# Latent attentions: value products in two parts over neighbouring tiles, values in three equal pieces, a key projection moved by one tile

## The chip, the cores and the metric

The kernel runs on one NeuronCore of a Trainium2 chip. What is compared is the time of one execution on the device, in microseconds (us). The figure for the kernel before is the median of three runs; the rows below come from one further execution, taken with the hardware profiler.

## The reference

A sequence of 1,024 tokens, with 16 meta tokens ahead of it (1,040 positions, padded here to 1,044), passes two layers of a first block and then one layer of a second block. Only the latent attention of the first block is touched by the change. Cut to what matters:

```python
def mla_mix(c_q, c_kv, k_r, ...):                 # 4 heads
    q = (rms_norm(c_q, q_norm_w) @ w_uq)          # per head 128 plain + 64 rotated columns
    kv = (rms_norm(c_kv, kv_norm_w) @ w_ukv)      # per head 128 key + 128 value columns
    k_nope, v = kv[..., :128], kv[..., 128:]
    k = concatenate([k_nope, broadcast(k_rope)])
    s = einsum('bqhd,bkhd->bhqk', q, k) * scale
    p = softmax(s)
    o = einsum('bhqk,bkhd->bqhd', p, v)           # the value product
for l in range(2):
    ...
    y_a = mla_mix(...)
    mix = concatenate([y_f * silu(f_gate), y_p * silu(p_gate), y_a * silu(a_gate)])
    h = h + mix @ w_out[l]
```

Everything is float32 in accuracy. A product of two float32 operands is made of three products of rounded parts, high by high, high by low and low by high; hence the names that end in `_hi` and `_lo`.

## The kernel before, in words

The function `latent_heads` (L1414) computes the attention of a layer. It is called once for each of the two layers and fills about a sixth of the program. The work is cut into tiles of 116 query rows (`HT`), 9 tiles to a head (`NH`), 4 heads, so 36 tiles to a layer. A chunk is 3 tiles, 348 positions (`CH1`); projections and value products are made chunk by chunk.

What each engine does for a tile `s` is written out by hand, in one loop over `s` on each engine. Each engine works off its own list strictly in the order written; semaphores tie the lists together.

- **TensorE** (`PE`): `score(s)` (L1468) makes 15 products for the scores of tile `s` over all keys, into three PSUM banks that exist once. Its first product waits until the exponential of the tile before has read them (`exp_done`). Then come the jobs of the tile (below), then `transposes(s - 1)` (L1515), 9 transposes of the probabilities of the tile before, again into three banks that exist once: they wait for `turned_saved`, which says that the last transposed tile has been copied out.
- **ScalarE** (`ACT`): the exponential of tile `s` (L1543), the high parts of the jobs' results (L1553 to L1559), then the high part of the transposed probabilities of tile `s - 1` (`pT_hi`, L1576).
- **VectorE** (`DVE`): the maximum of the scores of tile `s` and its negative (L1586, L1588), the rotation of query parts (L1594 to L1597), the reciprocal and the scaling of the probabilities (L1600, L1602), the low parts of the jobs' results (L1620) or, for a value product, its multiplication by the gate (L1608, tile `mix`, for the last head `last`), then the low part of the transposed probabilities (`pT_lo`, L1631).

A layer has 60 jobs beside the tiles: `kn` (a key projection of one chunk, 2 float32 products), `qn` and `qr` (plain and rotated query projection, 3 products each), `v` (values, several tiles of keys at a time), and `pv` (the value product of a chunk: 9 tiles of keys, 3 products each, 27 in all). `head_jobs` (L1386) is the table that gives the jobs of the tile with index `i` in head `n`. All jobs share two PSUM banks, 6 and 7, in turn; job `j` may start only when job `j - 2` has been saved (L1489, L1490):

```python
if j >= 2:
    pe.wait_ge(job_saved, j - 1)
```

The transposed probabilities of a chunk stand in one buffer, which exists once. ScalarE may write the first tile of the next chunk into it only when the value product of the last chunk has been made (L1574, L1575), where `x` is the tile whose transposes are copied out:

```python
if x % 3 == 0 and x:
    act.wait_ge(job_done, number["pv", (x - 1) // NH, (x - 1) % NH // 3] + 1)
```

`x` is 3 and 6 (index in the head) in the loop passes of tiles 4 and 7, where the table also has the value products of chunks 0 and 1. Chunk 2's stands in tile 1 of the next head.

Of the kernel before, what the change touches and what calls it, by code (L numbers as in the profile page):

```python
# [29 lines left out]
P = 128  # L30
# [16 lines left out]
MLA_HEADS = 4  # L47
MLA_SCALE = (128 + 64) ** -0.5
HALF = L1 // 2 + 1
HT = 116  # L50
NH = TP // HT
# [1334 lines left out]
def head_jobs(s):  # L1386


    n, i = divmod(s, NH)
    jobs = {0: [("kn", n + 1, 0), ("kn", n + 1, 1)], 1: [("pv", n - 1, 2)], 2: [("v", n, 0), ("v", n, 1)],  # L1390
            3: [("v", n, 2), ("qr", n, 2)], 4: [("qn", n, 2), ("pv", n, 0)], 5: [("qr", n + 1, 0)],
            6: [("qn", n + 1, 0)], 7: [("kn", n + 1, 2), ("pv", n, 1)], 8: [("qr", n + 1, 1), ("qn", n + 1, 1)]}
    return [job for job in jobs[i] if 0 <= job[1] < MLA_HEADS]


# [18 lines left out]
def latent_heads(core, io, layer, slots, mix, rope, wqk, ident, tensors, first_tile):  # L1414
# [4 lines left out]
    nc = core.nc  # L1419
    tiles = MLA_HEADS * NH  # L1420
    steps = range(-NH, tiles + 2)
    order = [job for s in steps for job in head_jobs(s)]
    number = {job: j for j, job in enumerate(order)}
    with_hi = [sum(job[0] != "pv" for job in order[:j]) for j in range(len(order) + 1)]
    ropes = [sum(job[0] == "qr" for job in order[:j]) for j in range(len(order) + 1)]

    t = tensors
# [13 lines left out]
        return (3 * n + c) % 2  # L1441

    def v_tiles(c):
        return slice(4 * c, min(4 * c + 4, NH))

    def v_bank(j, c):
        n = min(4, NH - 4 * c)
        return core.psum[0:HT, 6 + j % 2, 0:n * P].rearrange("p (t n) -> p t n", t=n)
    with core.phase("pads_set", "wqk_in2", "wqk_in3", "job_done", "job_hi", "job_saved", "qr_step",
                    "qr_ready", "scores_done", "max_ready", "bias_ready", "exp_done", "inv_done", "prob_ready",  # L1450
                    "turned_done", "turned_hi", "turned_saved") as \
# [11 lines left out]
        @block.tensor  # L1463
        def _(pe):
            def score(s):
                n, i = divmod(s, NH)
                if s == 0:
                    pe.wait_ge(pads_set, 1)  # L1468
                if i == 0:
                    pe.wait_ge(job_saved, number["kn", n, 2] + 1)  # L1470
                if i % 3 == 0:
                    pe.wait_ge(job_saved, max(number["qn", n, i // 3], number["qr", n, i // 3]) + 1)
                if s >= 1:
                    pe.wait_ge(exp_done, s)
                b = slot_of(n, i // 3)
                q = slice(i % 3 * HT, (i % 3 + 1) * HT)
                for part, (one, other) in enumerate((
                        (qn_hi[:, b, q], kn_hi[n % 2]), (qn_hi[:, b, q], kn_lo[n % 2]),
                        (qn_lo[:, b, q], kn_hi[n % 2]), (qr_both[:, b, q], kr_hi),
                        (qr_both[:, b, q], kr_lo))):  # L1480
                    for c in range(3):
                        w = min(CH1, L1 - c * CH1)
                        last = nc.tensor.matmul(scores[:, c, 0:w], one, other[:, c * CH1:c * CH1 + w],
                                                start=(part == 0), stop=(part == 4))
                last.then_inc(scores_done, 1)

            def work(job):
                kind, n, c = job
                j = number[job]  # L1489
                if j >= 2:  # L1490
                    pe.wait_ge(job_saved, j - 1)
                if kind == "kn" and c == 0 and n >= 2:
                    pe.wait_ge(wqk_in[n], 16)
                if kind == "pv":
                    pe.wait_ge(turned_saved, NH * n + 3 * c + 3)
                    pe.wait_ge(job_saved, number["v", n, 2] + 1)
                    for t in range(NH):
                        for part, (one, other) in enumerate(((v_hi, pT_hi), (v_hi, pT_lo), (v_lo, pT_hi))):
                            last = nc.tensor.matmul(bank(j), one[:, t, :], other[:, t, :],
                                                    start=(t == 0 and part == 0), stop=(t == NH - 1 and part == 2))  # L1500
                elif kind == "v":
                    for t in range(4 * c, min(4 * c + 4, NH)):
                        for k in range(2):
                            last = nc.tensor.matmul(core.psum[0:HT, 6 + j % 2, t % 4 * P:(t % 4 + 1) * P],
                                                    slots[:, CKV + k, t * HT:(t + 1) * HT],
                                                    wqk[n % 2][:, 3 + k, 128:256], start=(k == 0), stop=(k == 1))
                else:
                    k0, src, kt = (3, CKV, 2) if kind == "kn" else (0, CQ, 3)
                    cols = slice(128, 256) if kind == "qr" else slice(0, 128)
                    for k in range(kt):  # L1510
                        last = nc.tensor.matmul(bank(j), wqk[n % 2][:, k0 + k, cols], slots[:, src + k, chunk(c)],  # L1511
                                                start=(k == 0), stop=(k == kt - 1))
                last.then_inc(job_done, 1)

            def transposes(s):  # L1515
                pe.wait_ge(prob_ready, s + 1)
                if s >= 1:
                    pe.wait_ge(turned_saved, s)
                for t in range(NH):
                    last = nc.tensor.transpose(core.psum[0:HT, 3 + t // 3, t % 3 * HT:(t % 3 + 1) * HT],  # L1520
                                               prob[s % 2][:, t * HT:(t + 1) * HT], ident[0:HT, 0:HT])
                last.then_inc(turned_done, 1)
            for s in steps:
                if 0 <= s < tiles:
                    score(s)
                if s == tiles:
                    pe.wait_ge(exp_done, tiles)
                    first_tile.tensor(pe, range(0, 2))
                if s == tiles + 1:
                    first_tile.tensor(pe, range(2, 4))  # L1530
                for job in head_jobs(s):
                    work(job)
                if 1 <= s <= tiles:
                    transposes(s - 1)

        @block.scalar
        def _(act):
            for s in steps:
# [7 lines left out]
                for job in head_jobs(s):  # L1546
                    kind, n, c = job
                    j = number[job]
                    if kind != "pv":
                        act.wait_ge(job_done, j + 1)  # L1550
                    if kind == "qr":
                        act.wait_ge(qr_ready, ropes[j] + 1)
                        nc.scalar.activation(qr_both[0:64, slot_of(n, c), :], qa[:], ACT.Copy).then_inc(job_hi, 1)  # L1553
                    if kind == "qn":
                        nc.scalar.activation(qn_hi[:, slot_of(n, c), :], bank(j), ACT.Copy).then_inc(job_hi, 1)
                    if kind == "kn":
                        nc.scalar.activation(kn_hi[n % 2][:, chunk(c)], bank(j), ACT.Copy).then_inc(job_hi, 1)
                    if kind == "v":
                        nc.scalar.activation(v_hi[:, v_tiles(c), :], v_bank(j, c), ACT.Copy).then_inc(job_hi, 1)  # L1559
# [20 lines left out]
        def _(dve):  # L1580
            nc.vector.memset(core.psum[:, 2, L1 - 2 * CH1:CH1], MASKED).then_inc(pads_set, 1)
            for s in steps:
# [6 lines left out]
                for job in head_jobs(s):  # L1589
                    kind, n, c = job  # L1590
                    j = number[job]
# [11 lines left out]
                for job in head_jobs(s):  # L1603
                    kind, n, c = job
                    j = number[job]
                    if kind == "pv":
                        dve.wait_ge(job_done, j + 1)
                        nc.vector.tensor_tensor(mix[:, 4 + n, chunk(c)], bank(j), slots[:, A_GATE + n, chunk(c)],  # L1608
                                                ALU.mult).then_inc(job_saved, 1)
                        continue  # L1610
                    dve.wait_ge(job_hi, with_hi[j] + 1)
                    if kind == "qr":
                        lo, x, hi = (qr_both[64:P, slot_of(n, c), :], qa[:], qr_both[0:64, slot_of(n, c), :])
                    if kind == "qn":
                        lo, x, hi = qn_lo[:, slot_of(n, c), :], bank(j), qn_hi[:, slot_of(n, c), :]
                    if kind == "kn":
                        lo, x, hi = kn_lo[n % 2][:, chunk(c)], bank(j), kn_hi[n % 2][:, chunk(c)]
                    if kind == "v":
                        lo, x, hi = v_lo[:, v_tiles(c), :], v_bank(j, c), v_hi[:, v_tiles(c), :]
                    nc.vector.tensor_tensor(lo, x, hi.bitcast(F32), ALU.subtract).then_inc(job_saved, 1)  # L1620
# [3027 lines left out]
```

## Time and profile before

| what | value |
|---|---|
| median of 3 runs | 3171.22 us (3167.86 to 3183.21) |
| the profiled execution, its own time | 3170.96 us |
| its span in the profile | 3169.2 us |
| granted TensorE clock over the span | 0.984 of 2.4 GHz |
| the four heads of layer 1 in the trace | 281.5 to about 537 us |
| the four heads of layer 2 in the trace | about 888 to 1146 us |

Times in the rows are microseconds from the start of the span. TensorE's pass over an operand has two records, the load of the weights (PEld) and the product (PE); products are pipelined, so that one of 0.32 us follows the one before it by about half of that, and the beginnings, not the durations, are to be subtracted. What stands in brackets at a row's end is the idle time of the engine before it, and what ended it. PEclk is the share of full clock that was granted.

### The profile page before, as it was taken

The numbers are of one execution on the slowest core, as the hardware profiler recorded it, in microseconds if no ns is written. First come the engines' busy times: TensorE is split into PE (matmuls) and PEld (weight loads), VectorE is DVE, ScalarE is ACT, GpSimd is POOL, SyncE is SP. The second block draws the span as 40 slices with busy tenths as digits, with TensorE's granted clock in tenths as the row PEclk, the third lists the DMA queues.
The fourth block names the chain that finished last, engine by engine and source line by source line (L and its number), as shares of the span: only waits on it lengthen the run. The fifth ranks groups of instructions, "written<-read, shape, count | busy, mean of one in ns | idle before, by whom it ended". The sixth has DMA issues, their size and how long they took to land. (4 is left out here: it accounts for less than half of the span.)

```text
span 3169.2 us, 44449 instructions
## 1 busy us (share of the span) xinstructions
PE 2997.3 (95%) x18182; PEld 2558.4 (81%) x18182; DVE 2117.7 (67%) x2634; ACT 1067.5 (34%) x1555; POOL 961.7 (30%) x656
## 2 busy tenths in 40 slices
PE   7999998999999989998999898898999999999997
PEld 7997888999878888887876776666777886888875
DVE  5535765444366645998927756777957767877798
ACT  2012333201133423322012322666315453344534
POOL 2320000333100012553322532111333443454575
PEclk9999999999999999999999999999999999999998
DMA  4111000111100002433333004222533543555543
GB/s 143 45 36 43 23 1 7 62 61 47 55 9 23 1 21 67 149 117 114 103 129 125 8 35 117 75 67 71 208 131 97 189 158 119 163 166 173 163 149 120
DMA packets 114818, 284.38 MB, mean 90 GB/s; under 512 B 15238, under 2 KB 20998, under 8 KB 114600
## 3 DMA queue, kind: packets, MB, share of 16 engines
q1 hardware_dynamic: 111304, 276.83, 26.9%
q10 hardware_dynamic: 3312, 4.72, 0.4%
q8 instruction: 144, 2.36, 0.3%
q14 instruction: 58, 0.48, 0.0%
HBM read 239.47 MB, written 41.44 MB: 89 GB/s over the span
## 5 line engine op out<-in xcount | busy, mean ns | idle before, releaser
L4088 PE MATMUL psum<-x,w_hi 128*128 128x512 f32 x2016 | 626.9, 392 | 8.3 <-DVE x L4059 3.1
L199 POOL CAST w_hi<-w_raw 128x1024 fp32r<-128x1024 f32 x98 | 110.0, 1122 | 1554.6 <-PE psum L212 953.7
L4088 PEld LDWEIGHTS psum<-x,w_hi 128*128 128x128 f32 x2016 | 379.1, 189 | 93.0 <-issue 7.0
L4088 PE MATMUL psum<-x,w_lo 128*128 128x512 f32 x1008 | 393.5, 390 | 0.0
L3973 POOL TENSOR_TENSOR w_lo<-w_sum,w_hi 128x512 fp32r<-128x512 f32 x180 | 251.2, 1403 | 331.2 <-ACT w_hi L3967 331.2
L1061 PE MATMUL psum<-h,w_hi 128*128 128x512 f32 x1024 | 332.4, 406 | 20.2 <-PEq L126 8.5
L203 POOL TENSOR_TENSOR w_lo<-w_raw,w_hi 128x1024 fp32r<-128x1024 f32 x98 | 260.5, 2658 | 14.8 <-DVE y L1876 7.1
L1061 PEld LDWEIGHTS psum<-h,w_hi 128*128 128x128 f32 x1024 | 191.1, 193 | 70.4 <-issue 21.6
L4088 PEld LDWEIGHTS psum<-x,w_lo 128*128 128x128 f32 x1008 | 190.0, 188 | 39.9
L212 PE MATMUL psum<-hn_hi,w_hi 128*128 128x348 f32 x864 | 188.9, 327 | 18.0 <-DVE hn_lo L409 16.5
L1061 PE MATMUL psum<-h,w_lo 128*128 128x512 f32 x512 | 203.6, 398 | 0.0
L212 PE MATMUL psum<-hn_lo,w_hi 128*128 128x348 f32 x864 | 185.0, 323 | 0.0
L212 PE MATMUL psum<-hn_hi,w_lo 128*128 128x348 f32 x864 | 185.0, 322 | 0.0
L3967 ACT ACTIVATE w_hi<-w_sum 128x512 fp32r<-128x512 f32 x180 | 112.3, 630 | 207.8 <-DVE w_sum L3955 207.7
L212 PEld LDWEIGHTS psum<-hn_hi,w_hi 128*128 128x128 f32 x864 | 147.1, 190 | 21.3 <-issue 14.0
L1543 ACT ACTIVATE prob<-psum,softmax_small 116x1044 f32<-116x1044 f32 x72 | 81.5, 1132 | 208.2 <-DVE softmax_small L1588 208.2
L212 PEld LDWEIGHTS psum<-hn_lo,w_hi 128*128 128x128 f32 x864 | 146.9, 189 | 0.0
L212 PEld LDWEIGHTS psum<-hn_hi,w_lo 128*128 128x128 f32 x864 | 146.7, 190 | 0.0
L3955 DVE TENSOR_TENSOR w_sum<-w_raw 128x512 f32<-128x512 f32 x121 | 117.7, 976 | 29.8 <-PE psum L4088 22.3
L1511 PE MATMUL psum<-kept_slots,wqk 128*128 128x348 f32 x384 | 121.2, 457 | 5.3 <-PEq L126 3.2
L4121 DVE TENSOR_TENSOR hidden<-hidden,psum 128x1024 f32<-128x1024 f32 x64 | 76.4, 1215 | 63.5 <-ACT hidden L4114 41.9
L1061 PEld LDWEIGHTS psum<-h,w_lo 128*128 128x128 f32 x512 | 98.3, 192 | 21.7
(503 smaller groups left out, 6495.7 us busy)
## 6 DMA issues: line engine op xcount, KB each, us to landing
w_raw<-in_w_mlp SPq DMA_DIRECT2D x169, 256.0 KB, 2.9
norm_factor<-in_w_mlp SPq DMA_DIRECT2D x87, 256.0 KB, 2.8
w_raw<-in_w_mlp SPq DMA_DIRECT2D x42, 512.0 KB, 3.6
w_raw<-in_w_in SPq DMA_DIRECT2D x36, 512.0 KB, 3.6
w_raw<-in_w_gates SPq DMA_DIRECT2D x32, 512.0 KB, 4.0
gates_kept<-gate_stage SPq DMA_DIRECT2D x64, 256.0 KB, 2.2
gates<-gates_kept SPq DMA_DIRECT2D x32, 512.0 KB, 3.3
w_raw<-in_w_out SPq DMA_DIRECT2D x24, 512.0 KB, 3.7
```

What stands on the lines that cost most here:

```text
L199: self.core.nc.gpsimd.tensor_copy(self.hi[:, g % 2], self.raw[:, g % 2]).then_inc(self.hi_done, 1)
L203: self.core.nc.gpsimd.tensor_tensor(self.lo[:, g % 2], self.raw[:, g % 2], self.hi[:, g % 2].bitcast(F32), ALU.subtract) \
L212: last = nc.tensor.matmul(acc[:, c, :], w[:, g % 2, k, :], x(k)[:, c * ch:(c + 1) * ch], start=(k == 0 and part == 0), stop=(k == kt - 1 a ...
L1061: last = nc.tensor.matmul(self.core.psum[:, self.bank(x // KT), :], one[:, g % 2, k, :], other(k)[:, c * CH2:(c + 1) * CH2], start=(k == 0 ...
L1511: last = nc.tensor.matmul(bank(j), wqk[n % 2][:, k0 + k, cols], slots[:, src + k, chunk(c)], start=(k == 0), stop=(k == kt - 1))
L1543: nc.scalar.activation(prob[s % 2].rearrange("p (c n) -> p c n", c=3), scores, ACT.Exp, bias=nmx[:, s % 2:s % 2 + 1], scale=MLA_SCALE, acc ...
L3955: self.core.nc.vector.tensor_tensor(self.slot(self.core.weights.sums, j), raw[:, 0:4], raw[:, 4:8], self.SUMS[q]).then_inc(self.w_summed, 1)
L3967: self.core.nc.scalar.activation(self.slot(self.core.weights.hi, j), self.weight_source(j), ACT.Copy) \
L3973: self.core.nc.gpsimd.tensor_tensor(self.slot(w.lo, j), self.weight_source(j), self.slot(w.hi, j).bitcast(F32), ALU.subtract).then_inc(sel ...
L4088: last = self.core.nc.tensor.matmul(out, one[:, k, :], other[:, k, :], start=(group == 0 and k == 0 and part == 0), stop=(group == second ...
L4121: self.core.nc.vector.tensor_tensor(part, part, self.bank_pair(e), op).then_inc(self.added, 1)
```

## The change

1. The value products of chunks 0 and 1 of each head are made in two parts. `pv_begin` makes the first 15 of the 27 products, in the tile where all 27 stood (4 and 7); `pv` makes the last 12 in the next tile (5 and 8), first among that tile's jobs. Both parts have the same job number and the same bank; `pv_begin` waits for the bank and says nothing when it is done, `pv` reports. ScalarE and VectorE skip `pv_begin`; VectorE's multiplication by the gate moves with `pv`.
2. The values of a head are made in three pieces of 3 tiles of keys instead of 4, 4 and 1.
3. The key projection of chunk 2 of the next head (`kn`, 2) moves from tile 7 to tile 6.

The sequence of the job numbers and the wait in L1575 are as they were.

```diff
@@ head_jobs
-            3: [("v", n, 2), ("qr", n, 2)], 4: [("qn", n, 2), ("pv", n, 0)], 5: [("qr", n + 1, 0)],
-            6: [("qn", n + 1, 0)], 7: [("kn", n + 1, 2), ("pv", n, 1)], 8: [("qr", n + 1, 1), ("qn", n + 1, 1)]}
+            3: [("v", n, 2), ("qr", n, 2)], 4: [("qn", n, 2), ("pv_begin", n, 0)], 5: [("pv", n, 0), ("qr", n + 1, 0)],
+            6: [("qn", n + 1, 0), ("kn", n + 1, 2)], 7: [("pv_begin", n, 1)],
+            8: [("pv", n, 1), ("qr", n + 1, 1), ("qn", n + 1, 1)]}
@@ latent_heads
-    order = [job for s in steps for job in head_jobs(s)]
+    order = [job for s in steps for job in head_jobs(s) if job[0] != "pv_begin"]
     number = {job: j for j, job in enumerate(order)}
+    number.update({("pv_begin", n, c): number["pv", n, c] for n in range(MLA_HEADS) for c in range(2)})
...
     def v_tiles(c):
-        return slice(4 * c, min(4 * c + 4, NH))
+        return slice(3 * c, 3 * c + 3)
...
             def work(job):
                 kind, n, c = job
                 j = number[job]
-                if j >= 2:
+                begun = kind == "pv" and c < 2
+                if j >= 2 and not begun:
                     pe.wait_ge(job_saved, j - 1)
...
-                if kind == "pv":
+                if kind in ("pv_begin", "pv"):
                     pe.wait_ge(turned_saved, NH * n + 3 * c + 3)
                     pe.wait_ge(job_saved, number["v", n, 2] + 1)
-                    for t in range(NH):
+                    for t in range(5 if begun else 0, 5 if kind == "pv_begin" else NH):
                         for part, (one, other) in enumerate(((v_hi, pT_hi), (v_hi, pT_lo), (v_lo, pT_hi))):
                             last = nc.tensor.matmul(bank(j), one[:, t, :], other[:, t, :],
                                                     start=(t == 0 and part == 0), stop=(t == NH - 1 and part == 2))
...
-                last.then_inc(job_done, 1)
+                if kind != "pv_begin":
+                    last.then_inc(job_done, 1)
```

How the instructions move is seen at two places. The first is TensorE's list at tile 8 of the first head, from the last products of the scores to the transposes. L1484, L1501, L1513 and L1523 of the changed kernel are L1483, L1499, L1511 and L1520 of the kernel before. Before:

```order
L1483 MATMUL psum<-kr_lo,qr_both 116x344
L1511 MATMUL psum<-kept_slots,wqk_12 128x348 [waits job_saved_6]
L1511 MATMUL psum<-kept_slots,wqk_12 128x348 x2
L1511 MATMUL psum<-kept_slots,wqk_12 128x348 [waits job_saved_6]
L1511 MATMUL psum<-kept_slots,wqk_12 128x348 x2
L1520 MATMUL psum<-ident,prob 116x116 [waits turned_saved_6,prob_ready_6]
```

And now, from the last three of the 12 products of the second part on:

```order
L1501 MATMUL psum<-pT_hi,v_hi 128x348
L1501 MATMUL psum<-pT_lo,v_hi 128x348
L1501 MATMUL psum<-pT_hi,v_lo 128x348
L1513 MATMUL psum<-kept_slots,wqk_12 128x348 [waits job_saved_6]
L1513 MATMUL psum<-kept_slots,wqk_12 128x348 x2
L1513 MATMUL psum<-kept_slots,wqk_12 128x348 [waits job_saved_6]
L1513 MATMUL psum<-kept_slots,wqk_12 128x348 x2
L1523 MATMUL psum<-ident,prob 116x116 [waits turned_saved_6,prob_ready_6]
```

The second part of the value product now stands between the scores and the two query projections `qr` and `qn`; the wait of `qn` (the second `job_saved`) is for the job two before it, which is now the value product of the same tile. The second place is VectorE's list at the same tile. Before:

```order
L1586 TENSOR_REDUCE softmax_small<-psum 116x1 [waits scores_done_6]
L1588 TENSOR_SCALAR softmax_small<-softmax_small 116x1 [waits max_ready_6]
L1594 TENSOR_TENSOR rope_cos<-psum,norm_factor 64x348 [waits job_done_6]
L1595 TENSOR_TENSOR rope_sin<-psum,norm_factor 64x348
L1597 TENSOR_TENSOR rope_cos<-rope_cos,rope_sin 64x348 [waits qr_step_6]
L1600 RECIPROCAL softmax_small<-softmax_small 116x1 [waits exp_done_6]
L1602 TENSOR_SCALAR prob<-prob,softmax_small 116x1044 [waits inv_done_6]
L1620 TENSOR_TENSOR qr_both<-rope_cos,qr_both 64x348 [waits job_hi_6]
L1620 TENSOR_TENSOR qn_lo<-psum,qn_hi 128x348 [waits job_hi_6]
L1631 TENSOR_TENSOR pT_lo<-psum,pT_hi 116x9x116 [waits turned_hi_6]
```

And now:

```order
L1589 TENSOR_REDUCE softmax_small<-psum 116x1 [waits scores_done_6]
L1591 TENSOR_SCALAR softmax_small<-softmax_small 116x1 [waits max_ready_6]
L1597 TENSOR_TENSOR rope_cos<-psum,norm_factor 64x348 [waits job_done_6]
L1598 TENSOR_TENSOR rope_sin<-psum,norm_factor 64x348
L1600 TENSOR_TENSOR rope_cos<-rope_cos,rope_sin 64x348 [waits qr_step_6]
L1603 RECIPROCAL softmax_small<-softmax_small 116x1 [waits exp_done_6]
L1605 TENSOR_SCALAR prob<-prob,softmax_small 116x1044 [waits inv_done_6]
L1613 TENSOR_TENSOR mix<-psum,kept_slots 128x348 [waits job_done_6]
L1625 TENSOR_TENSOR qr_both<-rope_cos,qr_both 64x348 [waits job_hi_6]
L1625 TENSOR_TENSOR qn_lo<-psum,qn_hi 128x348 [waits job_hi_6]
L1636 TENSOR_TENSOR pT_lo<-psum,pT_hi 116x9x116 [waits turned_hi_6]
```

The multiplication by the gate, which saves the value product (`mix`, L1608 before, L1613 now), has come into tile 8, behind the exponential and the scaling of that tile.

## Rows read from the trace of the kernel before

**Rows 1.** Page, part 1: busy time, share of the span, instructions of each engine.

```profile
PE 2997.3 (95%) x18182; PEld 2558.4 (81%) x18182; DVE 2117.7 (67%) x2634; ACT 1067.5 (34%) x1555; POOL 961.7 (30%) x656
```

**Rows 2.** Waits of TensorE, heads 1 and 2 of layer 1: us, times, longest.

```profile
PE psum L1483 <- ACT prob L1543: 1.9, 4, 0.7
PE psum L1499 <- issue: 0.5, 2, 0.2
```

**Rows 3.** The same view, all four heads of layer 1.

```profile
PE psum L1483 <- ACT prob L1543: 10.3, 11, 1.9
```

**Rows 4.** Timeline, PE, first score products of tiles 4 to 9: start, us.

```profile
306.33 0.71 PE L1483 MATMUL psum<-kn_hi,qn_hi 128*116 128x348 f32 x3
...
315.64 0.72 PE L1483 MATMUL psum<-kn_hi,qn_hi 128*116 128x348 f32 x3
...
321.14 0.70 PE L1483 MATMUL psum<-kn_hi,qn_hi 128*116 128x348 f32 x3 [0.22 <-ACT prob L1543]
...
327.11 0.73 PE L1483 MATMUL psum<-kn_hi,qn_hi 128*116 128x348 f32 x3 [0.72 <-ACT prob L1543]
...
335.85 0.71 PE L1483 MATMUL psum<-kn_hi,qn_hi 128*116 128x348 f32 x3
...
342.65 0.72 PE L1483 MATMUL psum<-kn_hi,qn_hi 128*116 128x348 f32 x3
```

**Rows 5.** Timeline, PE, jobs and transposes of the same stretch.

```profile
318.10 1.92 PE L1511 MATMUL psum<-kept_slots,wqk 128*128 128x348 f32 x6
319.86 1.06 PE L1520 MATMUL psum<-ident,prob 116*116 116x116 f32 x9
...
331.07 0.32 PE L1499 MATMUL psum<-pT_hi,v_lo 116*128 116x348 f32 x1
...
335.03 1.05 PE L1520 MATMUL psum<-ident,prob 116*116 116x116 f32 x9
...
345.11 2.50 PE L1511 MATMUL psum<-kept_slots,wqk 128*128 128x348 f32 x8
347.45 1.06 PE L1520 MATMUL psum<-ident,prob 116*116 116x116 f32 x9
```

**Rows 6.** Timeline, ACT, tile 5 of head 0.

```profile
315.91 1.04 ACT L1576 ACTIVATE pT_hi<-psum 116x1044 fp32r<-116x1044 f32 x1 [2.62 <-PE psum L1520]
319.77 1.13 ACT L1543 ACTIVATE prob<-psum,softmax_small 116x1044 f32<-116x1044 f32 x1 [2.82 <-DVE softmax_small L1588]
```

**Rows 7.** Timeline, DVE, the same tile and the start of tile 6.

```profile
315.02 0.52 DVE L1608 TENSOR_TENSOR mix<-psum,kept_slots 128x348 f32<-128x348 f32 x1 [0.66 <-PE psum L1499]
316.99 1.25 DVE L1631 TENSOR_TENSOR pT_lo<-psum,pT_hi 116x1044 fp32r<-116x1044 f32 x1 [1.45 <-ACT pT_hi L1576]
318.30 1.25 DVE L1586 TENSOR_REDUCE softmax_small<-psum 116x1 f32<-116x1044 f32 x1
...
320.06 0.51 DVE L1594 TENSOR_TENSOR rope_cos<-psum,norm_factor 64x348 f32<-64x348 f32 x1 [0.32 <-PE psum L1511]
...
321.60 0.15 DVE L1600 RECIPROCAL softmax_small<-softmax_small 116x1 f32<-116x1 f32 x1
...
322.57 0.52 DVE L1620 TENSOR_TENSOR qr_both<-rope_cos,qr_both 64x348 fp32r<-64x348 f32 x1
323.22 1.25 DVE L1631 TENSOR_TENSOR pT_lo<-psum,pT_hi 116x1044 fp32r<-116x1044 f32 x1
324.38 1.24 DVE L1586 TENSOR_REDUCE softmax_small<-psum 116x1 f32<-116x1044 f32 x1
```

**Rows 8.** Busy time by stretch; length, busy PE, PEld, DVE, ACT, POOL; then PEclk.

```profile
292.52:300.85 8.33, 8.33 (x56) 8.33 (x57) 5.01 (x8) 3.20 (x5) 0.00 (x0) 0.80 0.00 0
356.29:363.03 6.74, 6.74 (x59) 6.74 (x58) 4.00 (x6) 3.35 (x5) 0.00 (x0) 1.00 0.00 0
286.00:293.30 7.30, 4.97 (x32) 4.18 (x31) 3.94 (x8) 3.81 (x7) 0.00 (x0) 1.00 0.00 0
468.00:476.00 8.00, 6.30 (x43) 5.81 (x42) 5.92 (x8) 2.47 (x4) 0.00 (x0) 1.00 0.01 2
```

More of the change, by code:

```diff
@@ L1443, in v_tiles @@
     def v_tiles(c):
-        return slice(4 * c, min(4 * c + 4, NH))
+        return slice(3 * c, 3 * c + 3)
     def v_bank(j, c):
-        n = min(4, NH - 4 * c)
-        return core.psum[0:HT, 6 + j % 2, 0:n * P].rearrange("p (t n) -> p t n", t=n)
+        return core.psum[0:HT, 6 + j % 2, 0:3 * P].rearrange("p (t n) -> p t n", t=3)
     with core.phase("pads_set", "wqk_in2", "wqk_in3", "job_done", "job_hi", "job_saved", "qr_step",
@@ L1501, in work @@
                 elif kind == "v":
-                    for t in range(4 * c, min(4 * c + 4, NH)):
+                    for t in range(3 * c, 3 * c + 3):
                         for k in range(2):
-                            last = nc.tensor.matmul(core.psum[0:HT, 6 + j % 2, t % 4 * P:(t % 4 + 1) * P],
+                            last = nc.tensor.matmul(core.psum[0:HT, 6 + j % 2, t % 3 * P:(t % 3 + 1) * P],
                                                     slots[:, CKV + k, t * HT:(t + 1) * HT],
@@ L1548, in _ @@
                     j = number[job]
-                    if kind != "pv":
+                    if kind not in ("pv_begin", "pv"):
                         act.wait_ge(job_done, j + 1)
@@ L1605, in _ @@
                     j = number[job]
+                    if kind == "pv_begin":
+                        continue
                     if kind == "pv":
```

## The prediction

> **What bounds the kernel now.** I read the page's busy shares first: TensorE is busy for 95% of the span, VectorE for 67% [rows 1]. The edit touches only the two attention stretches, so I then read who waits for whom there. In the two middle heads of layer 1 TensorE waits for the exponential pass for 1.9 us in all, four times [rows 2]; over the four heads it waits 10.3 us [rows 3], the rest lying where the first and last head have fewer jobs. So the middle of an attention is bound by TensorE, with hardly a gap to fill.
>
> Beside it runs a second bound, which the timeline shows. From one tile's first score product to the next's there is a closed ring: scores, maximum, exponential, next scores. At tile 5 it takes 321.14 - 315.64 = 5.50 us [rows 4] and TensorE waits at its end. Its parts: scores until 318.10 (2.46 us) [rows 4, 5], maximum from 318.30, exponential from 319.77 (1.47 later), next scores at 321.14 (1.37 later) [rows 4, 6, 7]. A tile takes whichever is longer, TensorE's own work or the ring. The ring also passes through queues that are strictly in order: the maximum stands behind VectorE's `pT_lo` of two tiles back, and the exponential behind ScalarE's `pT_hi` of that same tile. At tiles 5 and 8 these two passes belong to transposed tiles 3 and 6, and ScalarE's waits for the value product of the chunk before (L1575). Before the change that product is done in the tile before, ahead of the transposes, so the wait costs nothing: ScalarE's pass at 315.91 is released by the transposes [rows 6].
>
> The lengths of tiles 4 to 8 in the first head are 9.31, 5.50, 5.97, 8.74 and 6.80 us [rows 4], together 36.32.
>
> **Prices.** One value product takes (335.03 - 331.07)/25 = 0.158 us [rows 5], so the first part (15) is 2.38 us and the second (12) 1.90. A query projection is 319.86 - 318.10 = 1.76, a key projection (347.45 - 345.11)/2 = 1.17 [rows 5], the transposes 335.85 - 335.03 = 0.82 [rows 4, 5]. `pT_hi` leads `pT_lo` by 316.99 - 315.91 = 1.08 [rows 6, 7]; `pT_lo` leads the maximum by 324.38 - 323.22 = 1.16 where both are ready [rows 7], taken as 1.2.
>
> **The values in equal pieces.** TensorE's sum for tiles 2 and 3 is unchanged: 36 passes, four for each tile of keys, of which eight move from tile 2 to tile 3. Tile 2 takes 6.74 us with 32 of them [rows 8]; less scores and transposes that is (6.74 - 2.46 - 0.82)/32 = 0.108 each, so it shrinks to 5.9, still longer than the ring, and tile 3 grows by the same 0.86. ScalarE and VectorE copy as many elements as before. Cost: nothing, hidden under TensorE; if not hidden, a few tenths of a us per head either way.
>
> **Tile 4** loses the 12 products and stays bound by TensorE: 9.31 - 1.90 = 7.41. The change is -1.90.
>
> **Tile 5**, from its first score product: the scores end at 2.46, the 12 products at 4.36. Their last result and the semaphore take about 0.2, so ScalarE's `pT_hi` of tile 3 starts at 4.6; `pT_lo` 1.08 later at 5.7; the maximum of tile 5, queued behind it, at 6.9; the exponential 1.47 later at 8.35; the next scores 1.37 later at 9.7. That is +4.2 against 5.50. TensorE's own work there is 2.46 + 1.90 + 1.76 + 0.82 = 6.94, so it stands idle for 2.8 us: some 0.8 ahead of the transposes, which wait for `pT_lo` of tile 3, and 1.9 after them.
>
> **Tile 6** gets the key projection: 2.46 + 1.76 + 1.17 + 0.82 = 6.2, against 5.97 with its 0.72 of wait [rows 4]. The ring, behind VectorE's backlog from tile 5, needs about as long. The change is +0.2.
>
> **Tile 7** loses the key projection and the 12 products. But its first part waits for `pT_lo` of tile 5, behind the exponential of tile 6, reciprocal, scaling and two low parts on VectorE; by the same prices that is saved 3.15 us after the tile's start. Then 2.38 and 0.82: 6.4 us, against 8.74. The change is -2.3.
>
> **Tile 8** is the dear one. The exponential starts at 8.35, as in tile 5. VectorE meanwhile does the rotation for `qr`, 321.60 - 320.06 = 1.54 us [rows 7], after the negative at about 8.3, and comes to the reciprocal at 9.9. From there to the next pass it is 322.57 - 321.60 = 0.97 [rows 7], so the multiplication by the gate runs from 10.8 to 11.3 (0.52 long [rows 7]). Only that saves the value product, and `qn` waits for it: the same bank, the job two before. So TensorE does scores, 12 products and `qr` until 6.12 and then waits 5.2 us. `qn` takes 1.76 to 13.1, the transposes 0.82: 13.95 us, against 6.80. The change is +7.15. Behind `qn` are queued the transposes and the scores of the next head.
>
> A head with a successor: -1.90 + 4.2 + 0.2 - 2.3 + 7.15 = +7.35 us; there are 3 in each layer, 6 in all: +44.1. The last head has no projections for a next one: tile 4 -1.9, tile 5 +4.2, tile 6 0, tile 7 -1.9 and tile 8 +3.4 (the transposes of tile 7 wait for `pT_lo` of tile 6 until 6.9 instead of 3.5), +3.8; two of them: +7.6. The sum without the clock is +51.7 us. Nothing outside the two attentions can use the time, since the next products need the attention's result.
>
> **The clock.** No row shows an idle of 5.2 us in mid-attention, so I bound it. From 286.0 to 293.3 TensorE was busy for 4.97 of 7.30 us, and the stretch after it has a granted clock of 0.80 on average, that is 3.4 of 8.33 us at 1.2 instead of 2.4 GHz. It took 8.33 us, where the same tile of the next head took 6.74 at full clock: 1.6 us for one fall [rows 8]. From 468 to 476 it idled for 1.7 us and no fall came [rows 8]. So I count one fall for each of the six long idles, 6 x 1.6 = 9.6 (ends: 0, and two falls each, 19), and for the eight idles of 0.8 + 1.9 us in tile 5, which lie between the two rows, half a fall each of about 1 us, since the ring hides a part: 4 (ends 0 and 12.8). Together +13.6.
>
> The Trainium skill goes further: "TensorE: Matmul & The Clock Gate", section "A second HAM failure mode: psum-queue depth-cycling", says that small idles between groups of products that cycle through PSUM banks are frequent enough to swing the clock. By it each of the 14 idles brings a fall; the trace agrees with it at 286 us and not at 468.
>
> **The sum** against the profiled execution: 3170.96 + 51.7 + 13.6 = 3236.3 us, taken as **3236**. The median of the runs, 3171.22, stands 0.3 above the profiled one, which changes nothing. A measurement of this kernel can tell about 0.5%, 16 us.
>
> **The rivals.**
> - *Every idle brings a fall.* 14 x 1.6 = 22.4 instead of 13.6: 3170.96 + 51.7 + 22.4 = 3245. For it: the fall after only 1.0 and 1.9 us of idle. Against it: 468 us.
> - *No new falls*, or the ring hides them: 3223. Against it: the idle at tile 8 is far longer than any that kept the clock.
> - *The bank's wait does not bite.* If the value product were saved before the exponential, tile 8 would end with its ring at 9.7 and be +2.9 instead of +7.15: 6 x 4.25 = 25.5 less, and only the short idles left: 3170.96 + 26.2 + 4 = 3201. Against it: in VectorE's list the multiplication stands behind the scaling.
> - *It evens out and is not slower.* If the last 12 products were reported early enough for `pT_hi` and `pT_lo` to be through when the maximum is due, the moved work would fill the waits at tiles 6 and 7, 0.22 + 0.72 a head [rows 4]: 8 x 0.94 = 7.5 us less, 3163. It decides from the point where `pT_lo` of tile 3 ends before the scores of tile 5 do, at 2.5 us. My walk has it at 6.9, and the scores stand ahead of the products in TensorE's list, so 1.90 us of products alone put it out of reach. To be faster by over 0.5% all 20.6 us of waits in two layers [rows 3] would have to go: 3150.
> - *It does nothing:* products are only shifted and the waits fall in gaps: 3171.
>
> **How the numbers follow.** Forecast 0.55, all falls 0.18, no falls 0.13, bank harmless 0.07, not slower 0.04 with 0.02 of it faster by 0.5%, nothing 0.03. The first three hold 0.86 and run from 3223 to 3245. With an uncertainty of 0.5 us in the sum of each of 8 heads' walks and the double falls at the long idles I take 3214 to 3253. Slower 0.93, same 0.05, faster 0.02.
>
> **What would show it.** Right: tile steps of about 7.4, 9.7, 6.2, 6.4 and 14 us; TensorE idle over 5 us ahead of a query projection in tile 8, ended by VectorE's `mix`; ScalarE's `pT_hi` released by the value product, three more falls of PEclk a layer. Wrong: `qn` in tile 8 starting right behind `qr`, the maximum of tile 5 starting at 2.7 us, or the time coming from outside the attentions.

## The result, and the profile after

The changed kernel takes 3248.55 us (median of 4 runs, 3242.62 to 3250.62) against 3170.61 us for the kernel before (its three runs from above and a fourth), a ratio of 1.0238 with a 95% interval of 1.0221 to 1.0255. It is slower by 78 us. The forecast was 3236 us with a range of 3214 to 3253.

The page, parts 1 and 2: TensorE's busy share falls from 95% [rows 1] to 93%, and PEclk falls in three slices that were at 9. The PEclk row of before:

```profile
PEclk9999999999999999999999999999999999999998
```

And after:

```profile
PE 3033.0 (93%) x18182; PEld 2579.5 (79%) x18182; DVE 2110.6 (65%) x2634; ACT 1066.6 (33%) x1555; POOL 959.2 (30%) x656
...
PEclk9999998999999989999999899999999999999998
```

The instruction counts of the engines are those of before. What grew is waiting, and the time of the products that ran at half clock: TensorE's busy time rises from 2997.3 [rows 1] to 3033.0 us with the same 18182 products. Where the waiting lies the waits of TensorE say (us in total, times, longest), over the four heads of layer 1; [rows 3] is the answering row of before:

```profile
PE psum L1513 <- DVE mix L1613: 15.0, 3, 5.0
PE psum L1484 <- ACT prob L1546: 11.5, 8, 1.9
PE psum L1523 <- DVE pT_lo L1636: 7.5, 5, 2.6
```

The first row did not exist before: a projection (L1513) that waits for the multiplication by the gate (`mix`), three times a layer, 5.0 us each. The third is the transposes' wait for `pT_lo`, which before came once, 0.9 us long.

The timeline of PE, first score products of tiles 4 to 9 of the first head, answers to [rows 4]:

```profile
305.79 0.72 PE L1484 MATMUL psum<-kn_hi,qn_hi 128*116 128x348 f32 x3
...
313.44 0.71 PE L1484 MATMUL psum<-kn_hi,qn_hi 128*116 128x348 f32 x3
...
323.11 0.70 PE L1484 MATMUL psum<-kn_hi,qn_hi 128*116 128x348 f32 x3 [1.52 <-ACT prob L1546]
...
329.31 0.72 PE L1484 MATMUL psum<-kn_hi,qn_hi 128*116 128x348 f32 x3
...
335.46 0.71 PE L1484 MATMUL psum<-kn_hi,qn_hi 128*116 128x348 f32 x3
...
350.89 0.72 PE L1484 MATMUL psum<-kn_hi,qn_hi 128*116 128x348 f32 x3
```

Subtracted, and with those of the experiments read in the same way (first head of layer 1; where a fall of the clock makes heads differ, the range is given), in us:

| tile | before | forecast | after | no split | gate early | idle filled | other data | other data, gate |
|---|---|---|---|---|---|---|---|---|
| 4 | 9.31 | 7.4 | 7.65 | 9.56 | 7.67 | 7.67 | 7.66 | 7.66 |
| 5 | 5.50 | 9.7 | 9.67 | 5.47 | 9.67 | 9.66 | 6.93 | 6.94 |
| 6 | 5.97 | 6.2 | 6.20 | 6.19 | 6.19 | 6.20 | 6.89 | 6.44 |
| 7 | 8.74 | 6.4 | 6.15 | 8.03 | 5.97 | 6.14 | 6.35 | 6.33 |
| 8 | 6.80 | 13.95 | 15.43 to 16.51 | 6.80 | 9.71 | 13.98 | 12.07 to 13.79 | 8.71 |

A "fall", here and below, is a stretch in which the granted TensorE clock is 1.2 instead of 2.4 GHz.

Tile 5 on ScalarE and VectorE (timelines, to be read with [rows 6, 7]):

```profile
318.05 1.04 ACT L1579 ACTIVATE pT_hi<-psum 116x1044 fp32r<-116x1044 f32 x1 [5.04 <-PE psum L1501]
321.75 1.13 ACT L1546 ACTIVATE prob<-psum,softmax_small 116x1044 f32<-116x1044 f32 x1 [2.65 <-DVE softmax_small L1591]
```

```profile
319.12 1.25 DVE L1636 TENSOR_TENSOR pT_lo<-psum,pT_hi 116x1044 fp32r<-116x1044 f32 x1 [5.04 <-ACT pT_hi L1579]
320.29 1.24 DVE L1589 TENSOR_REDUCE softmax_small<-psum 116x1 f32<-116x1044 f32 x1
```

`pT_hi` of tile 3 starts 318.05 - 313.44 = 4.61 us into the tile and is now released by the value product (L1501), not by the transposes. `pT_lo` follows at 5.68, the maximum at 6.85, the exponential at 8.31. The prediction's walk through the tile had 4.6, 5.7, 6.9 and 8.35. TensorE's two idles of this tile, 0.80 and 1.52 us, are in its own rows, the first ahead of the transposes, the second (shown above, at 323.11) behind them:

```profile
320.52 1.08 PE L1523 MATMUL psum<-ident,prob 116*116 116x116 f32 x9 [0.80 <-DVE pT_lo L1636]
```

Tile 8 (it starts at 335.46), VectorE and TensorE:

```profile
343.61 0.15 DVE L1591 TENSOR_SCALAR softmax_small<-softmax_small 116x1 f32<-116x1 f32 x1
343.68 0.50 DVE L1597 TENSOR_TENSOR rope_cos<-psum,norm_factor 64x348 f32<-64x348 f32 x1
...
345.21 0.15 DVE L1603 RECIPROCAL softmax_small<-softmax_small 116x1 f32<-116x1 f32 x1
345.39 0.76 DVE L1605 TENSOR_SCALAR prob<-prob,softmax_small 116x1044 f32<-116x1044 f32 x1
346.18 0.52 DVE L1613 TENSOR_TENSOR mix<-psum,kept_slots 128x348 f32<-128x348 f32 x1
```

```profile
346.76 3.47 PE L1513 MATMUL psum<-kept_slots,wqk 128*128 128x348 f32 x6 [5.00 <-DVE mix L1613]
350.07 1.06 PE L1523 MATMUL psum<-ident,prob 116*116 116x116 f32 x9
```

The multiplication runs from 10.7 to 11.2 us into the tile, and `qn` starts at 11.3. But `qn` then takes 350.07 - 346.76 = 3.31 us, where three such products take 1.76 at full clock [rows 5]. Its stretch, in the view of busy times (length; busy PE, PEld, DVE, ACT, POOL; PEclk):

```profile
344.00:353.00 9.00, 6.24 (x28) 4.92 (x29) 4.37 (x9) 3.01 (x5) 0.00 (x0) 0.81 0.00 0
486.00:500.00 14.00, 8.89 (x39) 6.62 (x38) 8.23 (x13) 3.22 (x5) 0.00 (x0) 0.76 0.00 0
```

A mean granted clock of 0.81 over 9 us is 3.4 us at 1.2 GHz; 0.76 over 14 us is 6.7 us. The first is the first head's tile 8 (15.43 us), the second the third head's (16.47 us).

Over the whole span the 77.8 us divide as follows, by the first score product of each layer (281.52 and 888.52 before, 282.54 and 924.68 after) and the start of the last multiplication by the gate (540.99 and 1146.57 before, 577.15 and 1219.03 after): the first attention +35.1, the second +36.3, everything outside +6.4. Of the 6.4, 1.0 lie ahead of the first attention, nothing between the two (347.5 us in both), and 5.4 behind the second.

### The profile page after: what moved, and what is told of

It reads as the page before. It is cut to its first block and busy times, and to the rows that moved or that the text cites. A ratio compares the mean times of both kernels' runs of the same rounds, so it can differ in the third digit from the quotient of the medians.

```text
span 3247.0 us, 44465 instructions
## 1 busy us (share of the span) xinstructions
PE 3033.0 (93%) x18182; PEld 2579.5 (79%) x18182; DVE 2110.6 (65%) x2634; ACT 1066.6 (33%) x1555; POOL 959.2 (30%) x656
## 5 line engine op out<-in xcount | busy, mean ns | idle before, releaser
L1513 PE MATMUL psum<-kept_slots,wqk 128*128 128x348 f32 x384 | 133.3, 492 | 35.3 <-DVE mix L1613 30.0
L1636 DVE TENSOR_TENSOR pT_lo<-psum,pT_hi 116x1044 fp32r<-116x1044 f32 x72 | 89.5, 1244 | 101.7 <-ACT pT_hi L1579 101.2
L1513 PEld LDWEIGHTS psum<-kept_slots,wqk 128*128 128x128 f32 x384 | 74.6, 203 | 75.4 <-DVE mix L1613 33.3
```

The source lines that it names most:

```text
L1636: nc.vector.tensor_tensor(pT_lo[:, :, cols].rearrange("p (b t) n -> p b t n", b=3), turned, pT_hi[:, :, cols].rearrange("p (b t) n -> p b ...
```

## The experiments

The ratios are to the kernel before, in runs on the same chip; its medians there were 3171.83 (first four experiments), 3173.03 (next three) and 3172.44 us (the last), so medians of experiments that ran on different chips can be compared to within some 2.4 us.

**Neither value product split.** `head_jobs` with `pv` whole in tiles 4 and 7; equal value pieces and the moved key projection stay.

```diff
-            4: [("qn", n, 2), ("pv_begin", n, 0)], 5: [("pv", n, 0), ("qr", n + 1, 0)],
-            6: [("qn", n + 1, 0), ("kn", n + 1, 2)], 7: [("pv_begin", n, 1)],
-            8: [("pv", n, 1), ("qr", n + 1, 1), ("qn", n + 1, 1)]}
+            4: [("qn", n, 2), ("pv", n, 0)], 5: [("qr", n + 1, 0)],
+            6: [("qn", n + 1, 0), ("kn", n + 1, 2)], 7: [("pv", n, 1)],
+            8: [("qr", n + 1, 1), ("qn", n + 1, 1)]}
```

> The changed kernel without the split: value products whole in tiles 4 and 7, values in three equal pieces and the key projection in tile 6 as in the change. My theory: both of these are hidden or harmless. Tile 2 shrinks from 6.74 to about 5.9 us and tile 3 grows from 5.47 to 6.3; tile 6 becomes 6.2, tile 7 loses 0.5 to 1.2 us. Total 3165 to 3171 us. Rival: the equal pieces or the moved projection carry a part of the 78 us, the time is then clearly over 3180.

Measured: 3168.71 us, ratio 0.9986 (0.9977 to 0.9995). The other two parts of the change cost nothing together; the whole loss belongs to the split. Tile 2 is 5.87 to 5.93 (7.45 in the one head where the clock fell), tile 3 6.33 to 6.35. One small thing differs from the prediction: tile 4 takes 9.57 instead of 9.31. In tile 3 of the second head VectorE's low part of the third value piece has grown (the same row was 0.29 us long before, at 370.40, with `pT_lo` at 371.27):

```profile
370.33 0.56 DVE L1620 TENSOR_TENSOR v_lo<-psum,v_hi 116x384 fp32r<-116x384 f32 x1
...
371.46 1.25 DVE L1631 TENSOR_TENSOR pT_lo<-psum,pT_hi 116x1044 fp32r<-116x1044 f32 x1
```

In both kernels the value product of tile 4 starts 0.10 us behind the end of that `pT_lo`; 0.25 us a head are paid for the equal pieces.

**Only chunk 0 split (tiles 4 and 5).** The table as in the change for tiles 4 and 5, as above for tiles 7 and 8.

> Only chunk 0's value product is split, over tiles 4 and 5; the rest as in the run without a split. My theory: tile 4 about 7.65, tile 5 about 9.7, tile 8 stays 6.8 us; (7.65 - 9.31) + 4.2 = +2.5 us a head, 8 heads, +20 us, and 0 to 8 us of lower clock: 3186 to 3199 us. Rival (each split costs as much as the other): half of the 78 us, 3210.

Measured: 3195.97 us, ratio 1.0068 (1.0052 to 1.0083): +27 against the run without a split. Tiles 4 and 5 are 7.66 and 9.68, tile 8 stays at 6.79.

**Only chunk 1 split (tiles 7 and 8).** The other way round.

> Only chunk 1's value product is split, over tiles 7 and 8. My theory: tile 7 about 6.3, tile 8 near 14 us at full clock and 16 with the falls; 6 heads by +5.2 and 2 last heads by about +1.5 give +34, and the clock 6 x 2.1 = 13: 3210 to 3222 us. The sum of this and of the split of chunk 0, each less the run without a split, should be the change within 6 us. Rival (the ring alone counts, the bank's wait does not): tile 8 at 9.7 us, 3190.

Measured: 3223.91 us, ratio 1.0156 (1.0141 to 1.0172): +55 against the run without a split, some 2 us above what was expected. Tile 7 is 6.12, tile 8 between 15.5 and 16.6. The two splits add up to 82, the change to 80 (3248.55 - 3168.71). So the second costs twice the first, and the two add up.

**The gate's multiplication earlier.** On VectorE it is issued one loop pass before, ahead of `pT_lo`.

```diff
+                    if kind == "pv" and c < 2:
+                        continue
                     if kind == "pv":
                         dve.wait_ge(job_done, j + 1)
...
+                for kind, n, c in head_jobs(s + 1) if s < tiles else ():
+                    if kind == "pv" and c < 2:
+                        j = number[kind, n, c]
+                        dve.wait_ge(job_done, j + 1)
+                        nc.vector.tensor_tensor(mix[:, 4 + n, chunk(c)], bank(j), slots[:, A_GATE + n, chunk(c)],
+                                                ALU.mult).then_inc(job_saved, 1)
                 if 1 <= s <= tiles:
```

> The changed kernel, but on VectorE the multiplication by the gate that saves the value product of tile 5 or 8 stands ahead of pT_lo of two tiles back, right behind the product, instead of behind the scaling. My theory: the query projection of tile 8 no longer waits; tile 8 becomes bound by the ring at 9.7 us instead of 16, tile 5 stays at 9.7. 6 x 4.3 = 26 us and 6 clock falls of 2.1 us less, some 1 us a head back in tiles 0 and 1, where the next bound lies: 3204 to 3220 us. Rival (the tile is long because of the ring and the clock alone): tile 8 stays over 12 us and the time over 3235.

Measured: 3212.76 us, ratio 1.012 (1.0102 to 1.0138). Timeline of PE in tile 8, which starts at 335.83: `qr` and `qn` now follow without a gap (x12), and the tile ends with its ring at 9.71 us.

```profile
335.83 0.71 PE L1484 MATMUL psum<-kn_hi,qn_hi 128*116 128x348 f32 x3
...
340.22 3.68 PE L1513 MATMUL psum<-kept_slots,wqk 128*128 128x348 f32 x12
...
345.54 0.69 PE L1484 MATMUL psum<-kn_hi,qn_hi 128*116 128x348 f32 x3 [0.75 <-ACT prob L1546]
```

36 of the 78 us hang on that one place in VectorE's list, falls of the clock included: six tiles 8 are 6.4 us shorter, and tiles 0 and 1 of the next head take 0.5 us back. Tile 5 is unmoved at 9.67, so what is left there is the ring.

**The idle time of tile 8 filled.** 24 products whose results nobody reads, between `qr` and `qn`.

```diff
+                if kind == "qn" and c == 1 and n >= 1:
+                    pe.wait_ge(turned_saved, NH * (n - 1) + 7)
+                    for _ in range(24):
+                        nc.tensor.matmul(core.psum[0:HT, 3, 0:CH1], kr_hi[:, 0:HT], kr_lo[:, 0:CH1],
+                                         start=True, stop=True)
```

> The changed kernel with 24 extra products (results never read, into the bank of the transposes once it has been copied out) on TensorE between the two query projections of tile 8, six times in all. They take 24 x 0.158 = 3.8 us at full clock and fit into the wait of 5.0 us. My theory: tile 8 takes 16 us instead of 13.95 because of clock falls only; with TensorE kept busy the falls go, tile 8 becomes 14.0 to 14.4 us, 10 to 13 us less in all: 3234 to 3241 us. Rival (the 2.1 us are not the clock but further waits): tile 8 stays at 16 us or grows and the time stays at 3247 or more.

Measured: 3234.55 us, ratio 1.0196 (1.018 to 1.0211). Adding 144 useless products made the kernel 14 us faster than the change (13 us by the two ratios, whose intervals do not touch). Timeline of PE, tile 8 of the first head, up to the next head's first product:

```profile
336.59 0.71 PE L1484 MATMUL psum<-kn_hi,qn_hi 128*116 128x348 f32 x3
...
343.61 4.09 PE L1495 MATMUL psum<-kr_lo,kr_hi 128*116 128x348 f32 x24 [0.71 <-DVE pT_lo L1641]
347.89 2.02 PE L1518 MATMUL psum<-kept_slots,wqk 128*128 128x348 f32 x6 [0.19 <-DVE mix L1618]
349.75 1.06 PE L1528 MATMUL psum<-ident,prob 116*116 116x116 f32 x9
350.57 0.72 PE L1484 MATMUL psum<-kn_hi,qn_hi 128*116 128x348 f32 x3
```

`qn` still waits for `mix`, but now takes 349.75 - 347.89 = 1.86 us. All six tiles 8 lie between 13.94 and 14.00; the walk at full clock had 13.95.

**The second part reads other data.** Its moving operand is the key projection, and ScalarE waits for the first part. The weights of the last four tiles of keys of chunks 0 and 1 are thereby replaced.

```diff
+                    if begun:
+                        hi_, lo_ = (k[n % 2][0:HT, :].rearrange("p (t n) -> p t n", t=NC1) for k in (kn_hi, kn_lo))
...
-                if kind != "pv_begin":
-                    last.then_inc(job_done, 1)
+                last.then_inc(begun_done if kind == "pv_begin" else job_done, 1)
...
-                        act.wait_ge(job_done, number["pv", (x - 1) // NH, (x - 1) % NH // 3] + 1)
+                        if x % NH:
+                            act.wait_ge(begun_done, 2 * (x // NH) + x % NH // 3)
+                        else:
+                            act.wait_ge(job_done, number["pv", x // NH - 1, 2] + 1)
```

> The changed kernel, but the second part of a value product reads the high and low parts of the key projection instead of the transposed probabilities (so the last four tiles of keys of chunks 0 and 1 are not attended with the right weights), and ScalarE's pT_hi waits for the first part only. The number and form of all instructions stay. My theory: tile 5 falls from 9.7 to TensorE's own 6.9 us, tile 8 to about 12, since the query projection still waits for the multiplication behind the scaling; 8 x 2.7 + 6 x 4 and part of the falls less, some 1 us back in tile 6: 3200 to 3215 us. Rival (the long ring has another cause than the wait for the product): tile 5 stays at 9.7.

Measured: 3192.87 us, ratio 1.0068 (1.0051 to 1.0085), 7 us below the expected stretch. Tile 5 falls to 6.93, TensorE's own work:

```profile
314.13 0.71 PE L1484 MATMUL psum<-kn_hi,qn_hi 128*116 128x348 f32 x3
...
321.06 0.71 PE L1484 MATMUL psum<-kn_hi,qn_hi 128*116 128x348 f32 x3
```

Tile 8 is 12.07 and 12.12 in the two heads without a fall and 13.75 to 13.79 in the other four: the bank's wait is still there, shorter. Timeline of PE, the start of tile 8 and its `qn`:

```profile
334.30 0.71 PE L1484 MATMUL psum<-kn_hi,qn_hi 128*116 128x348 f32 x3
...
343.73 3.70 PE L1516 MATMUL psum<-kept_slots,wqk 128*128 128x348 f32 x6 [3.13 <-DVE mix L1618]
```

Why the time came out below the expected stretch was not tested. I had counted on more falls than the trace shows, and on 2.7 us less in each tile 5, where the two last heads, which have no projection in it, gain 4.2 (9.69 to 5.49).

**Other data, and the gate right behind the maximum.** In addition the multiplication stands behind the negative maximum of the same tile.

> As the run with other data, and VectorE's multiplication stands right behind the maximum of the same tile. My theory: with both waits gone nothing is left of the cost. Tiles 4 to 8 become 7.6, 6.9, 6.5, 6.4 and 8.7 us, each near TensorE's own work, and the time goes to that of the run without a split or a little below it: 3158 to 3172 us. Rival (splitting itself costs, by further accumulation or code): over 3180 us.

Measured: 3162.26 us, ratio 0.9975 (0.9959 to 0.9991). With both waits gone, the split kernel is no slower than the one before, but faster, by 8 us by the ratio. In the trace the two attentions together are 9.9 us shorter than before, 6.8 of them in the two last heads and 3.1 in the other six. Tile 8 is 8.71 us:

```profile
335.43 0.71 PE L1484 MATMUL psum<-kn_hi,qn_hi 128*116 128x348 f32 x3
...
344.14 0.71 PE L1484 MATMUL psum<-kn_hi,qn_hi 128*116 128x348 f32 x3
```

This is no kernel to use, since it computes something else; the same freedom with the right data needs a second buffer for the transposed probabilities, 2 x 9 x 348 x 4 = 25,056 bytes per partition, by my count. Whether it fits beside the tensors of this stage is not shown; it was not run.

**The key projection moved, alone.** The kernel before with the row of the table for tiles 6 and 7 changed.

```diff
-            6: [("qn", n + 1, 0)], 7: [("kn", n + 1, 2), ("pv", n, 1)], 8: [("qr", n + 1, 1), ("qn", n + 1, 1)]}
+            6: [("qn", n + 1, 0), ("kn", n + 1, 2)], 7: [("pv", n, 1)],
+            8: [("qr", n + 1, 1), ("qn", n + 1, 1)]}
```

> The kernel before with one part of the change alone: the key projection of chunk 2 in tile 6 instead of tile 7; values in pieces of 4, 4 and 1, value products whole. My theory, from the run without a split: there tile 4 took 9.57 us instead of 9.31, since the third value piece makes VectorE save pT_lo of tile 2 later, 0.25 us a head; without it tile 4 is 9.31 again, tile 6 stays 6.2 and tile 7 becomes 8.0 to 8.2. 6 heads x (-0.7 + 0.2) = -3 us and none of the 2 us of the pieces: 3165 to 3169 us, below both kernels. Rival (the moved projection is worth nothing, the gain of the run without a split came from the pieces): 3171 us, as the kernel before.

Measured: 3168.90 us, ratio 0.9991 (0.9981 to 1.0002). The steps are as expected (tiles 4, 6 and 7: 9.31, 6.19, 8.03), so 6 x 0.5 = 3 us are there in the trace; in the time they do not stand out from no change. The run without a split, whose interval ends at 0.9995, is the only kernel with the whole computation whose interval lies below both kernels, by about 0.14%.

## Why the prediction was right, and where it was short

The direction, the mechanism and the range held. By its steps:

- **What bounds.** The ring of scores, maximum and exponential, and its passage through `pT_hi` and `pT_lo`, is shown by the run with other data: with the wait for the second part gone, tile 5 goes from 9.67 to 6.93.
- **Tile 4:** forecast 7.41, measured 7.65. The 0.25 is the term "values in equal pieces, cost nothing", which was a little wrong: 8 x 0.25 = 2 us.
- **Tile 5:** forecast 9.7, measured 9.67. **Tile 6:** 6.2 and 6.19 at full clock. **Tile 7:** 6.4 and 6.15.
- **Tile 8:** forecast 13.95 at full clock, measured 13.94 to 14.00 once the clock is held up. The earlier multiplication shows that the bank's wait is real; the rival by which it does not bite (3201) is out.
- **The sum without the clock** was +51.7, and the trace bears it out where it can be read. At full clock tiles 4 to 8 of a head with a successor change by -1.65, +4.2, +0.2, -2.6 and +7.2 us, together +7.3 (forecast 7.35), and tiles 2 and 3 cancel. Two errors of a quarter of a us cancel in it, which was luck: tile 4 as above, and tile 7, where `pT_lo` of tile 5 was saved 2.8 us after the tile's start and not 3.15. The two last heads cannot be read so, since in the changed kernel their tile 6 and their end have falls in both layers; they grew by 6.6 and 7.9 us (forecast 3.8 each, without the clock). If the forecast's 3.8 is taken for them, the sum is 52.
- **The clock** is the term that was mis-sized: 13.6 us in all, 9.6 of them for tile 8 at 1.6 each. In the trace the attentions grew by 71.4 us, so that some 19 are left for the clock. Tile 8 lost (15.43 + 16.51 + 16.47 + 16.12 + 16.09 + 16.16) - 6 x 13.97 = 13.0 us of it, 2.2 each, because behind five of the six idles TensorE ran at 1.2 GHz for about 6.7 us, and only behind the first for 3.4. Filling the idle gave 14 us back. Twice the time at half clock did not cost twice as much: 2.1 to 2.5 us against 1.5. The rest, some 6 us, is by my estimate 5.5 us in the tiles 6 (forecast 4), if those of the last heads take 5.4 at full clock, and some 4 at the ends of the last heads, less 3.1 for two falls that only the kernel before had (tile 2 of the first head in one layer, tile 7 of a last head). One reading under this term was wrong: the idles ahead of the fall at 293 us were 0.44 and 1.89 us, and not 1.0 and 1.9; together they are the 2.33 us that the busy time gives.
- **Outside the attentions** I had nothing; the profiled execution has +6.4 us there, about half of the 12.5 us by which 3236.3 falls short of its 3248.82. Of it 5.4 lie behind the second attention, where all kernels do the same work. There the profiled executions of the ten kernels take 2021.4 to 2030.3 us (2022.6 before, 2028.0 after), and the run with the idle filled takes 1.2 us less than the kernel before. So this part varies by itself as much as it differs here; why it does stays open. Runs of the kernel before alone differ by 12 us and more, with granted clocks between 0.979 and 0.985.
- **Every idle brings a fall** (3245), the rival that went by the Trainium skill's "TensorE: Matmul & The Clock Gate", section "A second HAM failure mode: psum-queue depth-cycling", is nearest in time, but not in the place: of the six tiles 6 that follow a tile 5 with its idle and belong to a head with a successor, only one is long (7.74 against 6.19), and in the last heads both are (7.44 and 7.43 against 5.4). The trace agrees with it in part only.
- **Not slower** (3163) and **nothing** (3171) are out. That the kernel with both waits gone takes 3162.26 does not bear the first one out, for all that the numbers agree: it was to gain 0.94 us a head in the waits of tiles 6 and 7, where tiles 4 to 8 of that run are only 0.24 us a head shorter than before (36.08 against 36.32), and it needs the bank's wait removed too.

## What to carry to other kernels

When a job is cut in two and its end moves one step later, list what was behind its report before: here a pass on ScalarE that stands ahead of the next exponential in the same queue, and a bank that the job after next must get back. The place of the releasing instruction in the releasing engine's queue decides the price, more than the work that is moved; compare 9.71 with 13.98 us for one such place. And where a step is already closed by a ring shorter than TensorE's work, there is little to win by evening out TensorE's work: 1.9 us of waits over two heads was all there was.

## What the runs showed of the hardware

The waits of 5 us of TensorE cost more here than 5 us. Six of them, each with the projection and the transposes behind it, lost 13 us more to half clock; 24 products with no use in each gave 14 us back in the time (3248.55 against 3234.55), though they come to 24 x 0.17 = 4.1 us of TensorE's time each. Waits of 3.1 us at the same place (the run with other data) were followed by a fall in four of six tiles. Idles of 0.8 and 1.5 us with the transposes between them were followed by a fall in some tiles and not in others of the same kernel: in one of six in the changed kernel, in three of six in the run with the idle filled.
